# Activation highs and lows as one 512-column product in feed-forward and feature projections

## The reference, cut to what matters

```python
def swiglu(h, w_in, w_out):
    a, u = jnp.split(h @ w_in, 2, axis=-1)
    return (jax.nn.silu(a) * u) @ w_out
...
q, k, v, g = jnp.split(h @ w_in, ...)      # retention; likewise attention, the mixed layer, two expert layers
```

## Time and profile before

| | |
|---|---|
| median of three executions | 3978.19 us |
| profiled execution: the span, all that the page tells of its time | 3980.1 us |
| TensorE busy | 3754.4 us (94%) |
| VectorE busy | 2967.2 us (75%) |
| ScalarE busy | 1828.1 us (46%) |
| GpSimd busy | 346.3 us (9%) |
| read from memory | 738.53 MB, 186 GB/s over the span |
| mean granted TensorE clock over the span | 0.96 |

### The profile page before, as it was taken

How to read it: one execution, slowest core, us unless ns; L and a number is a source line. 1 busy time by engine, 2 the same in 40 slices (tenths; PEclk the granted TensorE clock), 3 DMA queues, 4 the chain that set the end, 5 groups by cost and what they waited for, 6 DMA issues and landing times. The chain is left out here.

```text
span 3980.1 us, 72107 instructions
## 1 busy us (share of the span) xinstructions
PE 3754.4 (94%) x29159; PEld 3408.9 (86%) x29159; DVE 2967.2 (75%) x5883; ACT 1828.1 (46%) x3704; POOL 346.3 (9%) x259
## 2 busy tenths in 40 slices
PE   6999899999799779999999999999999999999898
PEld 6997699998699769899999887898999988898798
DVE  7776677776687676987676956589776778688865
ACT  3444445444354444434444456444344444545443
POOL 0000000000000003840000000067200000000000
PEclk9999999999699889999999999899999999999899
DMA  8757376764267424434444453244444444577354
GB/s 321 275 222 287 132 281 220 282 224 171 96 253 271 150 73 159 159 124 167 168 169 169 155 191 143 85 170 143 144 170 168 167 165 166 207 289 281 143 182 147
DMA packets 119661, 745.30 MB, mean 187 GB/s; under 512 B 13857, under 2 KB 14273, under 8 KB 44833
## 3 DMA queue, kind: packets, MB, share of 16 engines
q1 hardware_dynamic: 118082, 737.57, 50.5%
q10 hardware_dynamic: 416, 2.06, 0.1%
q0 software_dynamic: 832, 1.06, 0.1%
HBM read 738.53 MB, written 1.05 MB: 186 GB/s over the span
## 5 line engine op out<-in xcount | busy, mean ns | idle before, releaser
L972 ACT ACTIVATE weights_high<-weight_ring 128x512 fp32r<-128x512 f32 x2248 | 1294.6, 624 | 1208.4 <-PE bank L200 900.2
L980 DVE TENSOR_TENSOR weights_low<-weight_ring,weights_high 128x512 fp32r<-128x512 f32 x2016 | 1298.5, 687 | 604.3 <-ACT weights_high L972 599.3
L200 PE MATMUL bank<-h_high,weights_high 128*128 128x256 f32 x4800 | 1374.2, 286 | 31.8 <-DVE h_low L711 10.4
L200 PE MATMUL bank<-h_low,weights_high 128*128 128x256 f32 x4800 | 1365.3, 284 | 0.0
L200 PE MATMUL bank<-h_high,weights_low 128*128 128x256 f32 x4800 | 1364.6, 284 | 0.0
L200 PEld LDWEIGHTS bank<-h_high,weights_high 128*128 128x128 f32 x4800 | 927.2, 193 | 50.8 <-issue 27.1
L200 PEld LDWEIGHTS bank<-h_low,weights_high 128*128 128x128 f32 x4800 | 927.7, 193 | 9.5 <-issue 0.9
L200 PEld LDWEIGHTS bank<-h_high,weights_low 128*128 128x128 f32 x4800 | 927.4, 193 | 0.0
L200 PE MATMUL acc<-weights_high,hidden_high 128*128 128x512 f32 x1552 | 613.3, 395 | 0.0
L200 PE MATMUL acc<-weights_low,hidden_high 128*128 128x512 f32 x1552 | 606.4, 391 | 0.0
L200 PE MATMUL acc<-weights_high,hidden_low 128*128 128x512 f32 x1552 | 604.3, 389 | 0.0
(11 more groups left out here) (328 smaller groups left out, 3466.8 us busy)
## 6 DMA issues: line engine op xcount, KB each, us to landing
weight_ring<-stream SPq DMA_DIRECT2D x574, 1024.0 KB, 4.8
h_feat<-slots SPq DMA_DIRECT2D x96, 512.0 KB, 5.8
h_tok<-slots SPq DMA_DIRECT2D x94, 512.0 KB, 5.7
work<-slots SPq DMA_DIRECT2D x26, 512.0 KB, 8.4
mod_sums<-biases SPq DMA_DIRECT2D x7, 1536.0 KB
h_feat<-rows SPq DMA_DIRECT2D x8, 512.0 KB, 4.2
work<-rows SPq DMA_DIRECT2D x7, 512.0 KB, 5.7
work<-biases SPq DMA_DIRECT2D x1, 1536.0 KB
```

The lines of the kernel that those rows point to most:

```text
L200: ins = self.nc.tensor.matmul(out, lhs, rhs, start=start, stop=stop)
L972: act.activation(k.w_hi[:, b, q * self.QUARTER:(q + 1) * self.QUARTER], self.raw(g, q), ACT.Copy).then_inc(k.highs_ready, 1)
L980: return eng.tensor_tensor(k.w_lo[:, b, w], self.raw(g, q), k.w_hi[:, b, w].bitcast(F32), ALU.subtract)
```

## The change

h_high and h_low become the two halves of one tensor h_split, 128 x 8 x 2 x 256, so that for one row block the highs and lows of all tokens are 512 columns side by side. A new function in_product makes an input half: for each row block, weights_high against those 512 columns into a whole bank (highs' result in the left half, lows' in the right half), and weights_low against h_high into the left half. Of three matmuls of 256 columns, one of 512 and one of 256 are left, with the two orders (both, rest) in the first block and (rest, both) in the others. The bank's halves have then to be added: ScalarE copies the right half to SBUF (`rests` in the feed-forward, the destination in the projection), VectorE adds the left half to it.

In TwoLayers each half now has a bank of its own (c mod 2 x 2 + part). After in(c, 0): Copy on ScalarE, add into sum_out on VectorE. After in(c, 1): Copy and silu (of sum_out) on ScalarE; on VectorE an add into product and the multiply. One iteration later: hidden_high by a Copy on ScalarE in place of VectorE's cast, hidden_low on VectorE. The gate rows move from after half 25 to after half 24, with TensorE's wait for their copy before half 26. In ToFeatureRows each half has its bank, a Copy on ScalarE and a multiply-add on VectorE.

```diff
-        self.h_hi = sb("h_high", [P, DC, S], F32R)
-        self.h_lo = sb("h_low", [P, DC, S], F32R)
+        self.h_split = sb("h_split", [P, DC, 2, S], F32R)
+        self.h_hi, self.h_lo = self.h_split[:, :, 0, :], self.h_split[:, :, 1, :]
...
+    def in_product(self, pe, bank, hi, lo):
+
+        k = self.k
+        for kk in range(DC):
+            self.need(pe, kk // 2)
+            w = slice(kk * P, (kk + 1) * P)
+            both = (bank, hi, k.h_split[:, kk, :, :].rearrange("p a t -> p (a t)"))
+            rest = (bank[:, 0:S], lo, k.h_hi[:, kk, :])
+            for out, a, x in (both, rest) if kk == 0 else (rest, both):
+                end = kk == DC - 1 and out is bank
+                mm = k.mm(out, a[:, w], x, start=kk == 0 and out is bank, stop=end, last=end)
+        return mm
...
-        self.gates_after, self.gates = 25, None
+        self.gates_after, self.gates = 24, None
+        self.gates_before = self.gates_after + 2
...
     def scalar_after(self, act, g):
         k = self.k
-        if g in self.hidden_at:
-            c = self.hidden_at[g]
+        kind, c, part = self.halves[g]
+        if kind == "in":
             act.wait_ge(k.banks_for_scalar.sem, k.banks_for_scalar.take())
-            if c >= 2:
-
-                act.wait_ge(k.vector_for_scalar.sem, k.vector_for_scalar.take())
-            act.activation(self.act_out[:, c % 2, :], k.bank[:, c % NB, 0:S], self.func).then_inc(
+            act.activation(self.rests[:, part, :], self.bank_of(c, part)[:, S:2 * S], ACT.Copy).then_inc(
                 k.scalar_for_vector.sem, k.scalar_for_vector.send())
-            if c == self.chunks - 1:
-                k.vector_for_scalar.skip(2)
+        if g in self.last_in:
+            act.wait_ge(k.vector_for_scalar.sem, k.vector_for_scalar.take())
+            act.activation(self.act_out[:, c % 2, :], self.sum_out, self.func).then_inc(
+                k.scalar_for_vector.sem, k.scalar_for_vector.send())
+        if g - 1 in self.last_in:
+            c = self.last_in[g - 1]
+            act.wait_ge(k.vector_for_scalar.sem, k.vector_for_scalar.take())
+            act.activation(k.g_hi[:, c % 2, :], self.product, ACT.Copy).then_inc(
+                k.scalar_for_vector.sem, k.scalar_for_vector.send())
...
     def vector_after(self, dve, g):
         k = self.k
-        if g in self.hidden_at:
-            c = self.hidden_at[g]
+        if g in self.first_in:
             dve.wait_ge(k.scalar_for_vector.sem, k.scalar_for_vector.take())
-            dve.tensor_tensor(self.product, self.act_out[:, c % 2, :], k.bank[:, c % NB, S:2 * S], ALU.mult).then_inc(
+            dve.tensor_tensor(self.sum_out, self.bank_of(self.first_in[g], 0)[:, 0:S], self.rests[:, 0, :],
+                              ALU.add).then_inc(k.vector_for_scalar.sem, k.vector_for_scalar.send())
+        if g in self.last_in:
+            c = self.last_in[g]
+            dve.wait_ge(k.scalar_for_vector.sem, k.scalar_for_vector.take())
+            dve.tensor_tensor(self.product, self.bank_of(c, 1)[:, 0:S], self.rests[:, 1, :], ALU.add).then_inc(
+                k.dve_step, 1)
+            dve.wait_ge(k.dve_step, k.step("dve"))
+            dve.wait_ge(k.scalar_for_vector.sem, k.scalar_for_vector.take())
+            dve.tensor_tensor(self.product, self.product, self.act_out[:, c % 2, :], ALU.mult).then_inc(
                 k.vector_for_scalar.sem, k.vector_for_scalar.send())
-            dve.wait_ge(k.vector_for_scalar.sem, k.vector_for_scalar.sent)
-            dve.tensor_copy(k.g_hi[:, c % 2, :], self.product).then_inc(k.dve_step, 1)
-            dve.wait_ge(k.dve_step, k.step("dve"))
+        if g - 1 in self.last_in:
+            c = self.last_in[g - 1]
+            dve.wait_ge(k.scalar_for_vector.sem, k.scalar_for_vector.take())
             dve.tensor_tensor(k.g_lo[:, c % 2, :], self.product, k.g_hi[:, c % 2, :].bitcast(F32),
                               ALU.subtract).then_inc(k.vector_for_tensor.sem, k.vector_for_tensor.send())
...
     def products(self, pe, g, hi, lo):
         k = self.k
-        j, two = g // 2, g % 2
...
+        if g >= NB:
+            pe.wait_ge(k.vector_for_tensor.sem, k.vector_for_tensor.take())
+        self.in_product(pe, k.bank[:, g % NB, :], hi, lo).then_inc(k.banks_for_scalar.sem, k.banks_for_scalar.send())
...
+    def scalar_after(self, act, g):
+        k = self.k
+        act.wait_ge(k.banks_for_scalar.sem, k.banks_for_scalar.take())
+        act.activation(self.dst[:, g, :], k.bank[:, g % NB, S:2 * S], ACT.Copy, scale=self.factor(g)).then_inc(
+            k.scalar_for_vector.sem, k.scalar_for_vector.send())
 
     def vector_after(self, dve, g):
...
+        dve.wait_ge(k.scalar_for_vector.sem, k.scalar_for_vector.take())
+        dve.scalar_tensor_tensor(self.dst[:, g, :], k.bank[:, g % NB, 0:S], self.factor(g), self.dst[:, g, :],
+                                 ALU.mult, ALU.add).then_inc(k.vector_for_tensor.sem, k.vector_for_tensor.send())
```

More of the change, by code:

```diff
@@ L1046, with __init__ @@
 class TwoLayers(SplitWeights):
-    def __init__(self, k, chunks, parts, func, act_out, product):
+    def __init__(self, k, chunks, parts, func, rests, sum_out, act_out, product):
         super().__init__(k)
         self.chunks, self.parts, self.func = chunks, parts, func
-        self.act_out, self.product = act_out, product
+        self.rests, self.sum_out, self.act_out, self.product = rests, sum_out, act_out, product
         k.acc_from = k.acc_filled.reserve(TT)
@@ L1063, in __init__ @@
         self.take_halves(len(self.halves))
-        self.gates_after, self.gates = 25, None
-        self.hidden_at = {g: c for g, (kind, c, part) in enumerate(self.halves)
-                          if kind == "in" and part == parts - 1}
+        self.gates_after, self.gates = 24, None
+        self.gates_before = self.gates_after + 2
+        self.last_in = {g: c for g, (kind, c, part) in enumerate(self.halves) if kind == "in" and part == parts - 1}
+        self.first_in = {g: c for g, (kind, c, part) in enumerate(self.halves) if kind == "in" and part == 0}
@@ L1069, in products, with bank_of @@
+    def bank_of(self, c, part):
+        return self.k.bank[:, c % 2 * 2 + part, :]
     def products(self, pe, g, hi, lo):
         k = self.k
[L1071 to L1084, removed]
-                pe.wait_ge(k.vector_for_tensor.sem, k.vector_for_tensor.take())
[L1086 to L1093, removed]
-                    if c == self.chunks - 1:
-                        mm.then_inc(k.acc_filled.sem, 1)
-            if self.gates is not None and g == self.gates_after:
-                pe.wait_ge(k.mod_used, self.gates.done)
-                for h in range(2):
-                    mm = gate_row(k, k.bank[:, 2 + h, :], self.gates.where, h)
-                mm.then_inc(k.banks_for_scalar.sem, k.banks_for_scalar.send())
@@ new lines, in products @@
+        kind, c, part = self.halves[g]
+        if self.gates is not None and g == self.gates_before:
+            pe.wait_ge(k.scalar_for_tensor.sem, k.scalar_for_tensor.take())
+        if kind == "in":
+            self.in_product(pe, self.bank_of(c, part), hi, lo).then_inc(
+                k.banks_for_scalar.sem, k.banks_for_scalar.send())
+        else:
+            if self.gates is None or g != self.gates_after + 1:
+                pe.wait_ge(k.vector_for_tensor.sem, k.vector_for_tensor.take())
+            for t in range(TT):
+                x_hi, x_lo = (x[:, c % 2, t * P:(t + 1) * P] for x in (k.g_hi, k.g_lo))
+                for h in range(2):
+                    w = slice(h * 512, (h + 1) * 512)
+                    for i, (x, a) in enumerate(((x_hi, hi), (x_hi, lo), (x_lo, hi))):
+                        end = c == self.chunks - 1 and i == 2
+                        mm = k.mm(k.acc[:, 2 * t + h, :], x, a[:, w], start=c == 0 and i == 0, stop=end,
+                                  last=end and h == 1)
+                if c == self.chunks - 1:
+                    mm.then_inc(k.acc_filled.sem, 1)
@@ L1102, in scalar_after @@
+        if self.gates is not None and g == self.gates_after:
+            pe.wait_ge(k.vector_for_tensor.sem, k.vector_for_tensor.take())
+            pe.wait_ge(k.mod_used, self.gates.done)
+            for h in range(2):
+                mm = gate_row(k, k.bank[:, 2 + h, :], self.gates.where, h)
+            mm.then_inc(k.banks_for_scalar.sem, k.banks_for_scalar.send())
     def scalar_after(self, act, g):
         k = self.k
-        if g in self.hidden_at:
-            c = self.hidden_at[g]
+        kind, c, part = self.halves[g]
@@ L1374, in __init__ @@
         super().__init__(k)
-        self.dst, self.pairs, self.scaled, self.scale = dst, chunks // 2, scaled, scale
+        self.dst, self.chunks, self.scaled, self.scale = dst, chunks, scaled, scale
         self.take_halves(chunks)
@@ L1391, in products, with factor @@
-        if two == 1:
-            done = k.banks_for_vector if j % 2 == 0 else k.banks_for_scalar
```

(9 more changed lines are left out.)

2 lines of the change are left out of this document (1 added, 1 removed).

## The result

The changed kernel takes 3952.39 us (median of four, 3950.50 to 3954.61) against 3978.24: ratio 0.9929, 95% interval 0.9910 to 0.9949, or 28 us less (20 to 36). Forecast were 3949 and a range of 3942 to 3967. Its profiled execution spans 3949.1 us.

The account below looks back on a forecast made before the run. TensorE's matmul spacing was taken to bound the feed-forwards; 35.8 - 3.6 - 1.5 - 1.0 - 0.5 - 0.3 = 28.9 us saved gave a median of 3949.3 us, range 3942 to 3967.

Parts of the forecast that it names:

- The bound: Feed-forward layers: TensorE's spacing of matmul starts sets the time, 8.48 us a chunk, becoming 8.27.
- The gain of a block: Changed row blocks: 360 ns becomes 227 + 120 = 347, so 13 ns each over 2752 blocks, 35.8 us.
- The dense stretch: Third block's first feed-forward, halves 50 to 66: VectorE nearly full, added work there gives back 3.6 us.
- first halves: First half of 11 stages, fed piece by piece by VectorE's h_low: 0.1 us each not gained, 1.0 us.
- the first layer's odds: First layer: gate rows move by a half, ScalarE's copies end about as TensorE asks; 0.3 us cost.
- Feature projections: Five projections, 640 blocks: 8.3 us gained if TensorE stays the bound; 0.5 us off for waits on DMA.
- the barriers: End of each feature projection: Copy then multiply-add stand before TensorE goes on, +0.3 us five times, 1.5 us.
- The row of 1.61 us: After the first projection: TensorE stalled 1.6 us by late lows, cited for the rival that waits eat half.
- Waits that eat half: Rival, chance 0.14: VectorE's and ScalarE's waits interlock where slots are dense, three layers gain nothing; 3963 us.
- VectorE as the bound everywhere: Rival, chance 0.07: VectorE bounds all layers with slots, 8.8 us a chunk; slower, 3997 us.
- all arrives: Rival, chance 0.07: dense-stretch lateness comes out of idle time behind it, first halves gain too; 3945 us.
- width without effect: Rival, chance 0.06: a 512 between two 256s costs 10 ns more, a block gives 3 ns; 3977 us, no change.

Follow-up runs that it names:

- spreading: Changed kernel with the modulation slots of the third block's first feed-forward in halves 8 to 44 and 45 to 66: median 3949.90 us, ratio 0.9927.
- its variant: Kernel before with slots of retention's token projection in halves 2 to 32 and the third block's first feed-forward's slots spread: ratio 1.0005.

## Why the prediction was right

- **The bound.** TensorE's spacing sets the feed-forwards: the layer without slots follows it fully, 4.06 us for 22 chunks. Right.
- **The gain of a block** was mis-sized: 13 ns forecast, 10.3 measured. By medians over the chunks of the layer without slots the input halves take 5.589 us for 5.753, and the output half, which was to stay as it was, 2.724 for 2.747. By the layer's length that is 0.184 us a chunk in place of 0.208: 24.3 us in place of 27.5. The plain sum of two steps failed by what 512s behind 256s cost more. The trace of before already had this: behind the 256s the first five 512s of its output halves take 233, 236, 228, 233 and 231 ns and only the later ones 227, so the width ahead does count at a seam, and for several matmuls. Neither the other order nor the other bank half recovers it.
- **The dense stretch:** 3.6 forecast, 2.9 measured, by the mechanism named; shown by spreading.
- **Feed-forwards otherwise:** 1.2 us of waits for the first output half in layers 2 to 4 (by the spacing of the matmuls 0.41 each, by the profile's rows 0.24 each) were missed: hidden_low was said to be made "some 4 us before use", and the first chunk, with the residual's operations, was not looked at. With some 1 us for first halves and the first layer's odds, which no run takes apart, 19.3 us in place of about 23.
- **Feature projections:** 8.3 less 1.0 (their first halves and waits on DMA) forecast, 7.0 measured; the barriers 1.9 for 1.5. Right.
- **The step left out** was what the earlier end of retention's projection does to the stage behind it. The row of 1.61 us was read only as a case for a rival. It is a stall on a transfer issued behind the barrier; with the new projection it was longer, and a stretch of half clock came with it: 2.5 to 3.1 us in the two profiles of the changed kernel, up to 4 in a variant. The sum has no term for it.
- **The sum.** 28.9 forecast, 21.6 by the stages, 28 (20 to 36) by the timing. The forecast mechanism gives the 21.6; that the median came within 3 us of the forecast is in good part luck, since some 6 us of the timed difference are in no term of the sum. They must lie in stages that the change doesn't touch. By the traces, all that is left of the span without the stages of the two gains and the two losses takes 2516 to 2531 us in the three profiles of the kernel before and its variant, and 2510 to 2529, median 2515, in the ten with the new feed-forward. These overlap, and single executions differ there by more than 10 us, so whether the 6 us are chance of the clock or something lasting stays open.
- **The rivals.** Waits that eat half, VectorE as the bound everywhere, all arrives, width without effect: none occurred. VectorE's loads of 92 to 94% were covered, as was argued; at 98% (dense stretch) and in the residual's halves they were not. The rival of the width rule was right in kind, with 2 to 3 ns a block in place of 10.

## What to carry to other kernels

Where the profile shows an engine back to back, take a change of its instructions from the steps between starts, and look in the old trace how the steps behind a change of width differ from the rest: here the mix cost 2 to 3 ns a pair more than the steps of each alone. Work moved to another engine was free here where that engine was then 92 to 94% busy, and not at 98%; look at each stretch by itself, the first chunk too. And look at the first stall behind each stage that gets faster: a transfer that can be issued only behind the barrier does not come sooner after it, and here it came later. To tell a few microseconds from the clock's chance, compare the lengths of stages and not the spans.

## What was not expected of the hardware

A matmul of 512 columns behind one of 256 with other weights takes 231 to 241 ns to the next start, against 227 in a run of its kind; the 256 behind it takes 112 to 120. Grouping moves this surcharge to the next few 512s instead of removing it. And the stall in retention's token projection was dearer than its length. In the three profiles with the old feature projection, where the matmul behind the stall starts 2.0 to 2.2 us after the one ahead of it, the granted clock stays at 1.00. In the six with the new one, where it starts 2.9 to 3.6 us after it, 3.4 to 6.8 us at the 1.2 GHz level begin around the end of the stall.
